# A hybrid decoder layer on one core: experts by four instead of two, half units of w_xo, and four moves in the order of the work

## The chip, the cores and the metric

The kernel is one program on one of the eight cores of a Trainium2 chip, written by hand: each engine (PE, which multiplies matrices; DVE, ACT and POOL, which work on elements; SP, which only issues DMAs here) has its own list of instructions, and they wait for each other by semaphores. The metric is the device time of one execution in microseconds (us), lower is better.

## The reference

One layer of a decoder over 256 tokens of width 1024, everything in fp32, then a last RMS norm:

```python
u = rms_norm(x);  proj = u @ w_in        # 8936 columns: z, xBC, dt, q, k, v, indexer, two gates
y_ssm = ssm_branch(...) @ w_ssm_out      # conv, chunked scan of 32 heads, gated norm with silu(z)
y_att = dsa_branch(...) @ w_att_out      # top 64 keys per query, 16 heads, one k/v head
x = x + (sigmoid(g_ssm) * y_ssm + sigmoid(g_att) * y_att) @ w_mix_out
x = x + cross_attention(rms_norm(x), rms_norm(mem), w_xq, w_xkv, w_xo)    # 4 heads, 256 memory rows
# experts: top 1 of 4 groups, top 2 of its 8 experts, for each token; 32 experts of 1024 x 512
for e in range(32):
    hid = silu(t @ w_e_gate[e]) * (t @ w_e_up[e])
    out = out + comb[:, e:e + 1] * (hid @ w_e_down[e])
x = x + out;  return rms_norm(x)
```

The weights of the experts are 32 x 3 x 2 MB, 201 MB of the 278 MB that the kernel reads.

## The kernel before

**Projections.** Each weight matrix outside the experts comes in units of 128 x 2048 fp32 (1 MB). A unit lands in one of 5 slots of `raw_w`, ACT copies it rounded into one of 3 slots of `hi_w` (L657), DVE subtracts and leaves the rest over the raw values in `lo_w` (L1005), and PE makes three products of the parts (`product`, L1577 to L1579). SP issues a unit when PE has left the one five before it; ACT splits when PE has left the one three before it. The list `units` is the order of the loads, the list `steps` the order of the products. A step is either feature-major (`fm_step`: 256 moving columns) or token-major (`tm_steps`: 512 columns, two tiles of tokens, used for mo, vx and xo, each in two column halves c). Steps alternate between PSUM banks 0 and 1 (`bank_no`), so a step waits until its second forerunner has been evacuated.

**The stages, in order:** k and small projections, convolutions and q, z with the attention, g (gates) with the scan of the heads, ao (attention out), so (scan out), kx, mo, vx, qx, the cross attention, xo, the router, the experts, the last norm.

**The gate stage.** In block b of 16, PE makes g_b, then the weighted sums of heads 2b and 2b+1 (L1763, L1764) with the masked decays `mdec`, which POOL multiplies (L631) after ACT's exponentials (L855). DVE adds the skip term (`y_out`), POOL multiplies with silu(z) (`gate_y`), ACT squares (`square_y`) and splits (`gated_hi`), DVE splits (`gated_lo`). PE sums four blocks of squares at a time with four matmuls on 32 columns of its array each (`sum_squares`, L1806). Behind the last block ACT squares and splits 14 and 15 and makes the sigmoid of the gates (L878), for which the first evacuation of ao (`att_gate`, L1273) waits. The normalised memory rows are turned by PE (`transposes_of(memn, i)`, L1591) inside ao, after steps 4 and 6.

**The experts.** `CAP = 64` token slots per expert and pass. A gather (L1990, L1974) multiplies the normalised rows with one-hot columns `S` for four experts at a time (a turn). A pair of experts is one step: gate and up (`first_layer`, L2007) with two matmuls on 64 array columns each, one per expert, beside each other; silu and product on ACT and DVE (L953, L1521); transposes (L2061); down (`second_layer`, L2038); then the result is split and added to the tokens' rows by `scatter` (L2024). If an expert has more than CAP tokens, DVE counts more passes (`passes`, L1488), and then all weights are loaded and used again. A group is half of one matrix for the two experts of a pair: two pieces of 1 MB, 96 groups in all. The ring has 9 slots of two pieces and one that is used once, made of regions that other stages have left. SP issues the first 20 pieces one by one when their regions are free (among them `over_ring`, which waits for the last unit in a slot), and each later one when PE has left the group nine turns before it (`group_used`).

## Time and profile before

| | us |
|---|---|
| median of three runs | 967.01 (966.19 to 968.02) |
| the profiled execution, its time | 967.55 |
| the profiled execution, its span | 965.80 |
| PE busy | 905.9 |
| DVE, ACT, POOL busy | 445.0, 315.7, 139.1 |
| moved by DMA | 277.61 MB |

The span is from the first to the last recorded instruction. Busy times of one engine are shares of that span; engines overlap. PE's busy time counts pipelined matmuls, which overlap each other too. An "idle before" is the time in which an engine had nothing running in front of an instruction, and behind it stands who released it. Where a row of a table of stages gives busy times, they are of PE, PEld (PE's weight loads), DVE, ACT and POOL, in this order; a granted clock of 1.00 is 2.4 GHz.

### The profile page before, as it was taken

What the parts mean: (1) busy time and instruction counts of PE and PEld (TensorE: products, weight loads), DVE (VectorE), ACT (ScalarE), POOL (GpSimd) and SP (SyncE); (2) the same over time, 40 slices, a digit from 0 to 9 for tenths busy, and PEclk for the clock granted to TensorE, in tenths of its full rate; (3) what the DMA queues carried; (4) which work ended last, traced back from release to release, by engine and by line L of the source; (5) the groups of instructions that cost most, each with busy time, mean ns of one, the idle gap of its engine ahead of it and who ended that gap; (6) DMA issues with size and microseconds to landing.
All of it is one profiled execution on the core that took longest, in us unless ns stands there. A gap on an engine that the chain in (4) does not pass through costs nothing.

```text
span 965.8 us, 13766 instructions
## 1 busy us (share of the span) xinstructions
PE 905.9 (94%) x5671; PEld 624.6 (65%) x5671; DVE 445.0 (46%) x801; ACT 315.7 (33%) x515; POOL 139.1 (14%) x131
## 2 busy tenths in 40 slices
PE   5999999998999999999998999999999988998896
PEld 5899998887889999788774433434343433433432
DVE  4899977677977763464453111212121211210212
ACT  5555676667675334454340000000000000000112
POOL 1002369837850000000000000000000000000000
PEclk9999999999999999999999999999999999999999
DMA  8655553344355769656289899999999999999994
GB/s 225 185 178 172 175 160 110 126 132 131 111 162 152 227 207 359 224 190 246 60 329 362 355 422 421 421 421 421 421 420 421 421 422 420 421 421 421 420 421 184
DMA packets 108728, 277.61 MB, mean 287 GB/s; under 512 B 12850, under 2 KB 76514, under 8 KB 84090
## 3 DMA queue, kind: packets, MB, share of 16 engines
q1 hardware_dynamic: 108522, 276.21, 75.7%
q8 instruction: 45, 0.74, 0.3%
q10 hardware_dynamic: 144, 0.52, 0.1%
q14 instruction: 17, 0.14, 0.0%
HBM read 275.54 MB, written 1.05 MB: 286 GB/s over the span
## 4 chain that ended last, share of the span: by engine, by line
PE 62%; DMA 12%; DVE 7%; SPq 7%; ACT 5%; POOL 4%; issue 3%; ACTq 0%; DVEq 0%; POOLq 0%
PE bank L2007 14%; DMA moe<-in_w_e_up_dram 11%; PE bank L1577 9%; PE bank L1579 9%; PE bank L1578 9%; PE bank L2038 8%; SPq L417 7%; DVE lo_w L1005 2%; PE bank L2024 2%; PE bank L1974 2%; ACT hi_w L657 2%; POOL work L631 2%; PE bank L1763 1%; DVE work L1181 1%; PE bank L1882 1%
## 5 line engine op out<-in xcount | busy, mean ns | idle before, releaser
L2007 PE MATMUL bank<-moe,xg 128*64 128x512 f32 x1008 | 224.9, 595 | 15.3 <-DMA moe<-in_w_e_up_dram 9.9
L1005 DVE TENSOR_TENSOR lo_w<-raw_w,hi_w 128x2048 fp32r<-128x2048 f32 (+1 forms) x68 | 156.8, 2311 | 60.6 <-ACT hi_w L657 60.2
L1577 PE MATMUL bank<-u_hi,hi_w 128*128 128x256 f32 x616 | 177.0, 287 | 0.3 <-DVE work L1182 0.3
L1579 PE MATMUL bank<-u_hi,lo_w 128*128 128x256 f32 x616 | 174.0, 283 | 0.0
L2007 PEld LDWEIGHTS bank<-moe,xg 128*64 128x64 f32 x1008 | 73.7, 137 | 149.5 <-issue 148.8
L1578 PE MATMUL bank<-u_lo,hi_w 128*128 128x256 f32 x552 | 156.0, 283 | 0.0
L657 ACT ACTIVATE hi_w<-raw_w 128x2048 fp32r<-128x2048 f32 (+1 forms) x68 | 127.7, 1880 | 32.5 <-PE bank L1579 29.5
L1577 PEld LDWEIGHTS bank<-u_hi,hi_w 128*128 128x128 f32 x616 | 117.8, 191 | 3.8 <-issue 3.4
L2038 PE MATMUL bank<-moe,moe_buf 128*64 128x512 f32 x512 | 114.3, 596 | 5.9 <-DVE xg L1501 4.7
L1579 PEld LDWEIGHTS bank<-u_hi,lo_w 128*128 128x128 f32 x616 | 117.9, 191 | 0.0
L961 ACT ACTIVATE y_pair_hi<-bank 128x512 fp32r<-128x512 f32 x32 | 19.1, 598 | 291.3 <-PE bank L2038 291.3
L1578 PEld LDWEIGHTS bank<-u_lo,hi_w 128*128 128x128 f32 x552 | 105.6, 191 | 0.0
L2038 PEld LDWEIGHTS bank<-moe,moe_buf 128*64 128x64 f32 x512 | 36.2, 137 | 74.5 <-issue 68.6
L1532 DVE TENSOR_TENSOR y_pair_lo<-bank,y_pair_hi 128x512 fp32r<-128x512 f32 x32 | 22.1, 692 | 116.9 <-ACT y_pair_hi L961 116.9
L1521 DVE SCALAR_TENSOR_TENSOR moe_buf<-moe_buf,st,bank 128x512 f32<-128x512 f32 x16 | 12.0, 747 | 110.6 <-PE bank L2007 103.5
L1509 DVE CAST ST<-bank 128x256 fp32r<-128x256 f32 x16 | 6.8, 425 | 104.2 <-PE bank L2016 104.2
L953 ACT ACTIVATE moe_buf<-bank 128x512 f32<-128x512 f32 x16 | 9.6, 597 | 128.2 <-PE bank L2007 128.2
L631 POOL TENSOR_TENSOR work<-work,cbm 128x384 f32<-128x384 f32 x32 | 40.4, 1284 | 12.5 <-ACT work L855 11.7
L1577 PE MATMUL bank<-a_hi,hi_w 128*128 128x256 f32 x128 | 36.7, 287 | 1.1 <-DVE gates L1273 1.1
L1577 PE MATMUL bank<-y_hi,hi_w 128*128 128x256 f32 x128 | 36.3, 284 | 0.0
L1578 PE MATMUL bank<-y_lo,hi_w 128*128 128x256 f32 x128 | 36.2, 283 | 0.0
L1579 PE MATMUL bank<-y_hi,lo_w 128*128 128x256 f32 x128 | 36.2, 283 | 0.0
(326 smaller groups left out, 1401.2 us busy)
## 6 DMA issues: line engine op xcount, KB each, us to landing
moe<-in_w_e_up_dram SPq DMA_DIRECT2D x64, 1024.0 KB, 26.0
moe<-in_w_e_down_dram SPq DMA_DIRECT2D x64, 1024.0 KB, 26.4
moe<-in_w_e_gate_dram SPq DMA_DIRECT2D x62, 1024.0 KB, 26.0
raw_w<-in_w_in_dram SPq DMA_DIRECT2D x34, 1024.0 KB, 5.5
raw_w<-in_w_ssm_out_dram SPq DMA_DIRECT2D x8, 1024.0 KB, 5.5
raw_w<-in_w_xkv_dram SPq DMA_DIRECT2D x8, 1024.0 KB, 6.3
raw_w<-in_w_att_out_dram SPq DMA_DIRECT2D x4, 1024.0 KB, 5.1
raw_w<-in_w_mix_out_dram SPq DMA_DIRECT2D x4, 1024.0 KB, 8.8
```

The lines of the kernel that those rows point to most:

```text
L417: sp.dma_start(moe_slot[s][a][:, :].rearrange("p (t n) -> p t n", t=t // 2), src)\
L631: nc.gpsimd.tensor_tensor(mdec[:, 2 * ((b + 1) % 2) + a, :], seg[:, 2 * (b % 2) + a, :], cbm[:, h // 8, :], ALU.mult).then_inc(m_ready, 1)
L657: nc.scalar.activation(hi_w[:, m % HI_RING, 0:w], raw_w[:, m % RING, 0:w], ACT.Copy)\
L1005: tt(lo_w[:, m % RING, 0:w], raw_w[:, m % RING, 0:w], hi_w[:, m % HI_RING, 0:w].bitcast(F32), ALU.subtract).then_inc(lo_done, 1)
L1532: tt(y_pair_lo[:, c, :], bank[2 + c][:, :], y_pair_hi[:, c, :].bitcast(F32), ALU.subtract).then_inc(m_ylo, 1)
L1577: mm(dst, left[0], right[0], start=first, stop=False)
L1578: mm(dst, left[0], right[1], start=False, stop=False)
L1579: return mm(dst, left[1], right[0], start=False, stop=last)
L1974: last = mm(bank[b0 + q % 2][:, 256 * (k % 2):256 * (k % 2) + 256], part[:, i, k, :], S[:, i, :, :], start=(i == 0 and part is xn_hi), sto ...
L2007: last = mm(ps[64 * a:64 * a + 64, :], xg[:, k, P * o + CAP * a:P * o + CAP * a + CAP], w[:, k % (KT // 2), :], start=(k == 0), stop=(k == ...
L2024: last = mm(acc_bank[i][c][:, :], ST[o][:, i, :], y[:, c, :], start=False, stop=False, skip_group_check=True)
L2038: last = mm(bank[2 + c][64 * a:64 * a + 64, :], hT[:, k, CAP * a:CAP * a + CAP], w[:, k % 2, 512 * c:512 * c + 512], start=(k == 0), stop= ...
```

## The change

- `CAP` is 32; four experts (a quad) are one step, each on 32 columns of PE's array; a turn is eight experts. A group is half a matrix for four experts, four pieces of 1 MB; there are 48. The ring counts single pieces: 18 slots and two used once, over the same regions.
- w_xo comes in eight half units (256 rows, 512 columns, 512 KB) that share two slots of `raw_w` and two of `hi_w`. The other three slots and one go to expert pieces before the second four half units are issued.
- The weighted sums of block b follow g_(b+1); `y_out`, `gate_y`, `square_y`, `gated_hi`, `gated_lo` and `sum_squares` each come a block later.
- The sigmoid of the attention's gates comes ahead of the last three squares. The sums of squares' end, the memory rows' norm and their transposes come later in ao and behind so0.
- The column halves c=1 of mo, vx and xo go to banks 4 and 5.

The diff, cut:

```diff
-CAP = 64
-PAIRS = EXPERTS // 2
+CAP = 32
+FOUR = P // CAP
+QUADS = EXPERTS // FOUR
+TURN = 2 * FOUR
...
 RING = 5
 HI_RING = 3
 N_PRM = 14
...
         conv_no = {s: n for n, s in enumerate(convolved)}
-        bank_no = [(n - CONV_0) % 4 if CONV_0 <= n < STEP["z0"] else n % 2 for n in range(len(steps))]
+        bank_no = [(n - CONV_0) % 4 if CONV_0 <= n < STEP["z0"] else 4 + n % 2 if s[:3] in ("mo1", "vx1", "xo1") else n % 2
...
                     LAST_STEP[f"{kind}{j}"] = f"{kind}{2 * j + 1}"
+        XO = len(units)
+        for c in range(2):
+            for q in range(4):
+                src = w_xo[0, 256 * q:256 * q + 256, 512 * c:512 * c + 512].rearrange("(t p) n -> p t n", p=P)
+                units.append((f"xo{c}{q}", src, 2))
...
+        def slots_of(n):
+
+            if n < XO:
+                return n % RING, n % HI_RING, 0
+            m = n - XO
+            return (XO + m // 2 % 2) % RING, (XO + m // 2 % 2) % HI_RING, UNIT // 2 * (m % 2)
+
...
+        def before_of(n, ring):
+
+            if n < XO:
+                return n - ring
+            return n - 4 if n >= XO + 4 else XO - ring + (n - XO) // 2
...
+            c, q = divmod(n - XO, 4)
+            if n < XO:
+                eng.wait_ge(proj_ready, STEP[LAST_STEP[units[n][0]]] + 1)
+            elif q < 3:
+                eng.wait_ge(xo_used, 3 * c + q + 1)
+            else:
+                eng.wait_ge(proj_ready, STEP[f"xo{c}1"] + 1)
+
+        OVER_RAW = ((12,), (13,), (10,), (11,), (14,))
+        OVER_HI = ((15,), (6,), (7,))
+        OVER_QX = (19,)
 
         block = ctx.enter_context(nc.Block())
...
+            def over_raw(slot):
+
+                wait_used(sp, max(n for n in range(len(units)) if slots_of(n)[0] == slot))
+                first_load(*OVER_RAW[slot])
+
+            def over_hi(slot):
+
+                wait_used(sp, max(n for n in range(len(units)) if slots_of(n)[1] == slot))
+                first_load(*OVER_HI[slot])
+
             for n, (name, src, k) in enumerate(units):
+                if n == XO + 4:
+                    for slot in range(XO + 2, XO + RING):
+                        over_raw(slot % RING)
+                    over_hi((XO + 2) % HI_RING)
+                    sp.wait_ge(xs_ready, NT * X_HEADS)
+                    first_load(*OVER_QX)
...
-            over_ring(5, 1, raw_slot=3)
-            sp.wait_ge(xs_ready, NT * X_HEADS)
-            first_load(9, 1)
-            over_ring(7, 0, raw_slot=4)
-            over_ring(6, 0, raw_slot=0)
-            over_ring(3, 1, hi_slot=2)
-            over_ring(6, 1, raw_slot=1)
-            over_ring(7, 1, hi_slot=0)
-            over_ring(3, 0, hi_slot=1)
-            over_ring(5, 0, raw_slot=2)
-            first_load(8, 0)
-            first_load(8, 1)
...
+            for k in range(2):
+                over_raw((XO + k) % RING)
+                over_hi((XO + k) % HI_RING)
+            first_load(16)
+            first_load(17)
...
-                turn = turn_of(g) - MOE_RING
-                sp.wait_ge(group_used, turn + 1 if turn < TENTH else turn + 2)
-                for a in range(2):
-                    load_part(turn_of(g) % MOE_RING, a, 2 * (g // 6) + a, *load_of(g // 6, g % 6))
+            first_load(18)
+            for p in range(MOE_RING + len(ONCE), FOUR * MOE_GROUPS):
+                before = turn_of(p) - MOE_RING
+                before = before if before < ONCE[0] else before + len(ONCE)
+                sp.wait_ge(group_used, before // FOUR + 1)
+                first_load(p)
...
-                    gate_y(b - 1)
-            gate_y(SSM_HEADS // 2 - 1)
+                if b >= 2:
+                    gate_y(b - 2)
+            for b in range(SSM_HEADS // 2 - 2, SSM_HEADS // 2):
+                gate_y(b)
 
...
-                square_y(b - 2)
                 if b >= 3:
-                    gated_hi(b - 3)
+                    square_y(b - 3)
+                if b >= 4:
+                    gated_hi(b - 4)
             split_hi_through(UN["ao0"] + 2)
+            wait_evac(act, "g15")
+            nc.scalar.activation(gates[:, 8:16, :], gates[:, 8:16, :], ACT.Sigmoid).then_inc(gsig, 1)
+            square_y(13)
+            gated_hi(12)
             square_y(14)
             gated_hi(13)
             square_y(15)
-            wait_evac(act, "g15")
-            nc.scalar.activation(gates[:, 8:16, :], gates[:, 8:16, :], ACT.Sigmoid).then_inc(gsig, 1)
             gated_hi(14)
...
+            transposed_hi(u_hi, tiles=(0,))
...
+                if b == 1:
+                    transposed_hi(u_hi, tiles=(1,))
...
-                if b >= 1:
-                    y_out(b - 1)
+                if b >= 2:
+                    y_out(b - 2)
                 if b % 2 == 0:
                     split_lo_through(UN[f"g{b // 2}"] + 2)
-                if b >= 4:
-                    gated_lo(b - 4)
+                if b >= 5:
+                    gated_lo(b - 5)
+            y_out(14)
+            split_lo_through(UN["ao0"] + 2)
             y_out(15)
-            split_lo_through(UN["ao0"] + 2)
-            for b in range(12, 16):
+            for b in range(11, 16):
...
                 att_gate(b)
-                if b == 1:
+                if b == 3:
 
                     dve.wait_ge(ssq_mm, 4)
                     nc.vector.tensor_copy(rs_bc, bank[2][:, 0:SEQ]).then_inc(ssq_rows, 1)
-                if b == 2:
+                if b == 4:
+                    norm_rows(1, memx, memn)
+                if b == 5:
                     dve.wait_ge(ssq_mm, 5)
                     link(ts_(rs_bc, bank[2][:, SEQ:2 * SEQ], 1.0 / (32 * D_INNER), EPS, ALU.mult, ALU.add))
                     nc.vector.reciprocal(rs_bc, rs_bc).then_inc(gn_ms, 1)
-                if b == 3:
-                    norm_rows(1, memx, memn)
-                if b == 5:
-                    columns_of(0, g_mem, u_hi, m_lo)
-                if b == 7:
-                    columns_of(1, g_mem, u_hi, m_lo)
+            columns_of(0, g_mem, u_hi, m_lo)
...
+                if b == 0:
+                    columns_of(1, g_mem, u_hi, m_lo)
...
-            split_lo_through(UN["vx10"])
+            split_lo_through(UN["vx11"])
...
+            def state_sums(b):
+
+                pe.wait_ge(m_ready, 2 * b + 2)
+                if b >= 2:
+                    pe.wait_ge(y_used, b - 1)
+                else:
+                    pe.wait_ge(pv_lo, 7 + b)
+                for a in range(2):
+                    h = 2 * b + a
+                    last = weighted_sum(bank[6 + b % 2][64 * a:64 * a + 64, :], xdt[:, 0, HEAD * h:HEAD * h + HEAD],
+                                        xdt[:, 1, HEAD * h:HEAD * h + HEAD], mdec[:, 2 * ((b + 1) % 2) + a, :])
+                last.then_inc(y_ready, 1)
...
-                                        xdt[:, 1, HEAD * h:HEAD * h + HEAD], mdec[:, 2 * ((b + 1) % 2) + a, :])
-                last.then_inc(y_ready, 1)
-                if b in (6, 10, 14):
-                    sum_squares((b - 6) // 4)
-
+                    state_sums(b - 1)
+                if b in (7, 11, 15):
+                    sum_squares((b - 7) // 4)
+            state_sums(15)
 
             for b in range(8):
                 if b % 2 == 0:
                     w = use_unit(f"ao{b // 2}")
                 fm_step(f"ao{b}", w, P * (b % 2), a_parts)
-                if b == 1:
+                if b == 3:
                     sum_squares(3)
...
+                if b == 5:
                     pe.wait_ge(ssq_rows, 1)
                     mm(bank[2][:, SEQ:2 * SEQ], ones[:, :], rs_bc, start=True, stop=True).then_inc(ssq_mm, 1)
-                if b == 4:
+                if b == 7:
                     pe.wait_ge(gn_ms, 1)
                     transposes_of(memn, 0)
-                if b == 6:
-                    transposes_of(memn, 1)
 
...
                 w = use_unit(f"so{b}")
                 fm_step(f"so{b}", w, 0, y_parts, 16)
+                if b == 0:
+                    transposes_of(memn, 1)
 
             pe.wait_ge(tr_evac, 8)
...
 
-            for c in range(2):
-                tm_steps("mo", c, a_parts, mix_lo, (4, 8))
+            tm_steps("mo", 0, a_parts, mix_lo, (4, 8))
+            pe.wait_ge(seg_ready, 32)
...
+            def cross_output(c):
+
+                for q in range(4):
+                    w = use_unit(f"xo{c}{q}")
+                    pe.wait_ge(xo_lo, 2 + q // 2 * 2)
+                    if c == 1 and q == 2:
+                        for i in range(NT):
+                            rows_turned(0, i)
+                    for i in range(NT):
+                        if q == 0:
+                            bank_of(f"xo{c}{i}")
+                        for k in range(2):
+                            last = product(bank[bank_no[STEP[f"xo{c}{i}"]]][:, :],
+                                           [x[:, 2 * q + k, P * i:P * i + P] for x in a_parts],
+                                           [x[:, k, :] for x in w], q == 0 and k == 0, q == 3 and k == 1)
+                        if q == 3:
+                            last.then_inc(proj_ready, 1)
+                    if q < 3:
+                        last.then_inc(xo_used, 1)
+
...
+                    places = [where(off + h, a) for a in range(FOUR)]
+                    for s, landed_at in places:
+                        pe.wait_ge(moe_landed[s], landed_at)
                     for k in range(KT // 2 * h, KT // 2 * h + KT // 2):
                         if rows_at is not None and k in rows_at:
                             pe.wait_ge(m_xg, rows_at[k])
-                        for a in range(2):
-                            w = moe_slot[s][a][:, :].rearrange("p (t n) -> p t n", t=KT // 2)
-                            last = mm(ps[64 * a:64 * a + 64, :], xg[:, k, P * o + CAP * a:P * o + CAP * a + CAP],
-                                      w[:, k % (KT // 2), :], start=(k == 0), stop=(k == KT - 1))
+                        for a in range(FOUR):
+                            w = moe_piece[places[a][0]].rearrange("p (t n) -> p t n", t=KT // 2)
+                            last = mm(ps[CAP * a:CAP * a + CAP, :], xg[:, k, P * o + CAP * a:P * o + CAP * a + CAP],
```

## Rows read from the trace of the kernel before

**Rows 1.** The page's slices, 24.1 us each: what the DMAs moved.
```profile
GB/s 225 185 178 172 175 160 110 126 132 131 111 162 152 227 207 359 224 190 246 60 329 362 355 422 421 421 421 421 421 420 421 421 422 420 421 421 421 420 421 184
```

**Rows 2.** Stages: from:to, length, busy (count) per engine, granted clock, DMA share, GB/s.
```profile
463.50:495.90 32.40, 30.99 (x146) 25.46 (x145) 14.47 (x26) 10.57 (x18) 0.00 (x0) 1.00 0.41 144
495.90:511.70 15.80, 15.21 (x92) 11.26 (x90) 11.97 (x35) 8.02 (x10) 0.00 (x0) 0.89 1.01 417
511.70:545.00 33.30, 30.92 (x149) 12.04 (x150) 7.74 (x32) 2.39 (x4) 0.00 (x0) 1.00 0.85 332
545.00:951.00 406.00, 383.09 (x1872) 166.03 (x1870) 74.70 (x143) 27.86 (x45) 0.00 (x0) 1.00 1.01 420
```

**Rows 3.** SP in order of time: start, length, DMAs issued.
```profile
515.34 4.24 SPq L417 DMA_DIRECT2D moe<-in_w_e_down_dram  x4
...
523.07 11.98 SPq L417 DMA_DIRECT2D moe<-in_w_e_gate_dram  x4
```

**Rows 4.** The chain that ended last: start, length, what.
```profile
915.71 27.06 DMA moe<-in_w_e_up_dram
...
952.80 3.67 PE bank L2038 x16
```

**Rows 5.** Line 417, which issues the expert pieces: time to landing.
```profile
DMA to landing us min/median/max: 5.0/26.1/29.6
```

**Rows 6.** PE in order of time, four places.
```profile
241.34 0.64 PE L1806 MATMUL bank<-work,ones 128*32 128x256 f32 x8
...
506.01 1.10 PE L1949 MATMUL bank<-xres,ident 128*128 128x512 f32 x2
...
511.65 7.09 PE L2007 MATMUL bank<-moe,xg 128*64 128x512 f32 x32
...
528.01 0.75 PE L2061 MATMUL bank<-ident,moe_buf 128*128 128x128 f32 x4 [1.55 <-DVE moe_buf L1521]
```

**Rows 7.** PE in order of time, after the 14th pair.
```profile
899.56 0.39 PE L1974 MATMUL bank<-S,xn_hi 128*128 128x256 f32 x1 [2.71 <-DVE S L1407]
...
903.66 0.28 PE L1974 MATMUL bank<-S,xn_lo 128*128 128x256 f32 x1
```

**Rows 8.** Table of stages as in rows 2, four more stretches.
```profile
213.00:281.00 68.00, 63.97 (x539) 55.45 (x535) 57.05 (x120) 47.07 (x85) 55.86 (x45) 1.00 0.34 109
300.00:350.00 50.00, 50.00 (x419) 49.94 (x418) 36.33 (x47) 19.38 (x18) 0.00 (x0) 1.00 0.64 190
475.00:485.00 10.00, 10.00 (x46) 8.28 (x45) 3.94 (x3) 3.50 (x5) 0.00 (x0) 1.00 0.39 125
900.00:905.00 5.00, 5.00 (x31) 4.93 (x29) 2.08 (x3) 0.00 (x0) 0.00 (x0) 0.66 1.01 421
```

**Rows 9.** What PE waited for: total us, times, longest us.
```profile
PE bank L1763 <- POOL work L631: 3.8, 5, 1.5
...
PE bank L1577 <- DVE xres L1314: 2.5, 3, 0.8
...
PE bank L1591 <- issue: 1.5, 1, 1.5
...
PE bank L1577 <- DVE lo_w L1005: 0.5, 1, 0.5
```

**Rows 10.** ACT and PE between g15 and ao2, in order of time.
```profile
283.68 1.28 ACT L878 ACT_TABLE_LOAD   x1
...
284.97 1.92 ACT L878 ACTIVATE gates<-gates 128x2048 f32<-128x2048 f32 x1
...
288.68 0.36 PE L1577 MATMUL bank<-a_hi,hi_w 128*128 128x256 f32 x1 [1.11 <-DVE gates L1273]
```

**Rows 11.** Issues by line: size, us to landing.
```profile
xdt<-in_mem_dram SPq DMA_DIRECT2D x2, 512.0 KB, 4.2
```

**Rows 12.** Groups, xo stage: busy us, mean ns of one, idle before.
```profile
L1005 DVE TENSOR_TENSOR lo_w<-raw_w,hi_w 128x2048 fp32r<-128x2048 f32 x2 | 4.6, 2292 | 3.7 <-ACT hi_w L657 3.7
...
L657 ACT ACTIVATE hi_w<-raw_w 128x2048 fp32r<-128x2048 f32 x2 | 3.8, 1905 | 0.0
```

More of the change, by code:

```diff
@@ L391, in hybrid_block, with landed_sem @@
         FIRST_STEP.update({f"so{j}": f"so{j}" for j in range(8)})
-        FIRST_STEP.update({f"{k}{j}{h}": f"{k}{j}{h}" for k in ("vx", "mo", "xo") for j in range(2) for h in range(2)})
+        FIRST_STEP.update({f"{k}{j}{h}": f"{k}{j}{h}" for k in ("vx", "mo") for j in range(2) for h in range(2)})
+        def landed_sem(n):
+            return landed[n % RING] if n < XO else xo_landed[(n - XO) % 4]
         def landed_value(n):
+            if n >= XO:
+                return 16 * ((n - XO) // 4 + 1)
             return 16 * (n // RING + 1) + (16 * (len(PIECES[n % RING]) - 1) if n % RING < len(PIECES) else 0)
@@ L652, in split_hi_through, with transposed_hi @@
                     m = split[0]
-                    act.wait_ge(landed[m % RING], landed_value(m))
+                    act.wait_ge(landed_sem(m), landed_value(m))
                     if m >= HI_RING:
-                        wait_used(act, m - HI_RING)
-                    w = unit_len(m)
-                    nc.scalar.activation(hi_w[:, m % HI_RING, 0:w], raw_w[:, m % RING, 0:w], ACT.Copy)\
-                        .then_inc(hi_done, 1)
+                        wait_used(act, before_of(m, HI_RING))
+                    nc.scalar.activation(hi_at(m), raw_at(raw_w, m), ACT.Copy).then_inc(hi_done, 1)
                     split[0] += 1
             group = [0]
-            def transposed_hi(dst, between=None):
-                for i in range(NT):
+            def transposed_hi(dst, between=None, tiles=range(NT)):
+                for i in tiles:
                     for q in range(2):
@@ L1622, in tm_steps @@
                         pe.wait_ge(sem, halves[half])
-                    if half == 1 and between is not None:
-                        between()
                     for i in range(NT):
```

251 lines of the change are left out of this document (124 added, 127 removed).

## The prediction

> **What bounds the kernel now.** I read the busy slices of the page first, then the table of stages, then what PE waited for, then the two ends of the expert stage in order of time. The slices show the DMA rate: uneven between 60 and 359 GB/s in the first 21, and 420 to 422 from the 24th to the 39th [rows 1]. So there are two programs in one. Until about 511.7 us PE is the bound: it is busy nearly all the time and the DMA share is low, except in the last 16 us before the experts, where the ring of expert weights is filled at 417 GB/s. From 545 to 951 us the DMA engines are full (share 1.01, 420 GB/s) [rows 2], whatever PE does. A piece of expert weights is 1.0486 MB, so at 420.5 GB/s one lands every 2.494 us; there are 32 x 3 x 2 = 192 of them, before and after.
>
> That gives the end as a sum of three terms. T0 is when PE begins the first expert (511.65 [rows 6]). The ring holds 20 pieces, all issued by then; the other 172 can only start when PE gives a slot back, first at 515.34 [rows 3]. The last piece: the chain shows the third half-group from the end landing at 915.71 + 27.06 = 942.77, four pieces later is 952.8, and PE starts its last half-group at 952.80 [rows 4]. From there to the end of the span are 13.0 us.
> From 515.34 to 952.8 are 437.5 us for 172 x 2.494 = 428.9 us of transfer. The rest is 8.5 us: 2.5 us are the latency of one piece (its shortest landing is 5.0 us [rows 5], less 2.5 of transfer), and about 6.1 us are DMA engines idle for want of a free slot. The stage 511.7 to 545 shows it: 332 instead of 420 GB/s for 33.3 us is 7.0 us short, some of it before 515.34 [rows 2]. PE is the cause: two half-groups of two experts take 7.09 us (x32), then it waits 1.55 us for the product, and SP sits until 535 over four pieces [rows 3, 6].
>
> **The change part by part.**
> *Experts by four.* The number of matmuls stays, but each drives 32 columns of the array, not 64, and four can run beside each other. What the rows say on that: alone, an fp32 matmul over the whole array and 512 moving columns is two instructions in 1.10 us, some 0.9 without the drain; of those on 64 columns, 16 (x32) take 7.09, 0.443 each. So two do run beside each other, a pair in 0.886. Four 32-column ones already exist: the squares' sums at 241.34, four matmuls of 256 moving columns in 0.64 us with the drain [rows 6]. One after another they would take 4 x 0.44 = 1.8 us. So four run together, and I take 4 x 0.886 = 3.55 us for a half-group of four experts, the time that two experts had. The other end is two by two, 7.1 us.
> The Trainium skill's page TensorE: Matmul & The Clock Gate (part 3, measured speedup) has three column tiles at 2.38 times one, not 3; by that ratio a half-group would be 4.5 us and the result some 2 us later. The row of the four sums is the better witness here.
> In the steady part this buys nothing: PE needs for four experts 4 x 3.55 + 7.1 for the layers, some 5 for slots, transposes and scatters, and a gather of 3.9 every second time, about 28 us in 59.8 of DMA. Where PE was nearly as slow as the DMA, it now has half its time over. At the start it buys the idle time: at T0 + 3.7 as before, but then four slots (10 us of transfer) come free for every 3.6 us of PE. SP never starves again: ring 18, four pieces landed and in work, 14 outstanding, minus 1.5 landed before the next four are issued. **-6.1 us**, bounds -6.1 and 0.
> *The tail.* PE will now wait some 6 us before each half-group (10 us of DMA, 3.6 of work). After 2.71 us of idle time at 899.56 the granted clock was 0.66 over the next 5 us [rows 8], and the gather's matmuls took about 0.4 instead of 0.28 until about 903.5 [rows 7]: about 4 us at the 1.2 GHz level. While DMA is the bound that is free: even a whole half-group at half rate is 7.1 us, under 10. But the last one is behind the last piece: 4 us at half rate do 2 us of work, the rest 1.6: 5.6 instead of 3.6, **+2.0 us**; bounds 0 and +5.5 (all of it and the scatters at half rate).
> That an idle PE falls to the lower clock is also what the Trainium skill says (TensorE: Matmul & The Clock Gate, part 1, HAM oscillation); by that rule this change, which makes PE idle by design, pays at the end, and the row agrees.
> *Weighted sums a block later.* PE waited 3.8 us for POOL's product in the gate stage [rows 9]. POOL is busy 55.9 of 68 us there [rows 8], so it is no bound, only late by a part of a step; one more fm step (24 matmuls at 50/419 us, 2.9 us [rows 8]) in front covers the longest wait (1.5). Left open by it is the end of the stage: the last sums stand bare behind g15, y_out(15) stands behind a split of w_att_out, and the chain ACT split 1.9, table load 1.3, sigmoid 1.9, the squares and copies of 13 to 15 (seven at about 0.45), DVE's last lows and att_gate(0), 0.9, is 9.0 us [rows 10, 12]; PE's work between g15 and ao2 is 7.3 (sums 0.9 and 0.6, two steps of 2.9), so the wait of 1.1 becomes about 1.7, though the sigmoid now comes first: DVE waits for the last lows all the same. Of 3.8 + 1.1 + the short 0.4 I keep 0.7 in the blocks and 1.7 here: **-2.9 us**, bounds 0 and -5.3.
> *Memory rows turned later.* The 1.5 us before L1591 [rows 9] was the chain square root, scaling, transposes; it now has two to three more ao steps. **-1.5 us**, bounds 0 and -1.5. The second half behind so0 lies in 5.8 us steps and delays nothing.
> *Second halves in banks 4 and 5.* Three waits of 0.8 us for a residual addition (the rows' 2.5 [rows 9]) go, in mo, vx and xo; the new wait for seg_ready is long past. With the split of vx11 ahead of the columns the 0.5 us for lo_w goes too. **-3.0 us**, bounds 0 and -3.0.
> *Half units of w_xo.* Eight loads of 512 KB in place of four of 1024; c=1 reuses the slots of c=0, so each is issued when PE has left its forerunner. PE spends 12 x 10/46 = 2.6 us on a half unit [rows 8], so a load has three of them, 7.8 us. It needs a landing (512 KB of mem: 4.2 us [rows 11]), ACT's copy (half of 1.9) and DVE's subtraction (half of 2.3) [rows 12]: 6.3, slack 1.5. ACT and DVE sit on the half units with the norm's squares and the residual additions queued behind them; for xo12 the additions then come at the moment PE wants them for the transposes. I take **0**, bounds 0 and +4 (1 us for each of four). What it buys is five expert pieces issued before the second half rather than after; the ring was full at T0 anyway, so this only protects the smaller T0.
> *Router and tables.* Later passes have seven entries, not three, and the slot weights four copies: about 1.5 us more on DVE, which had 3 us to spare before the first slots are turned. Nothing.
>
> Sum: -2.9 - 1.5 - 3.0 = -7.4 on T0, -6.1 behind it, +2.0 at the end: -11.5. The profiled execution took 967.55 us (span 965.80), the median of the three runs is 967.01; so 967.55 - 11.5 = 956.05, less 0.54: **955.5 us**.
>
> **Rivals.** (1) *PE's gains before T0 are given back*: POOL and DVE at 82 and 84% of the gate stage become the pace, or the w_xo half units come late. For it: DVE's busy time there is 57.1 of 68 [rows 8]. Then -7.4 becomes -1 to -3: 960 to 962. (2) *The lower clock holds through the end*: +5.5 instead of +2.0, 959. Against it: the row recovers in about 4 us of work. (3) *Four tiles run two by two*: half-groups take 7.1 us, the 6.1 us stay lost and the last half-group costs 3.6 more, so 967.0 - 7.4 + 3.6 + 3 for the later first release: about 966, no change. Against it: the 0.64 us. (4) *A second pass, the slower side*: a pass now serves 32 tokens of an expert, not 64, and one expert with 33 makes every weight come again: 192 x 2.494 = 479 us, so 1434 us. It decides at one token: routing the reference's own inputs (its default draw) gives 512 places over 32 experts, 16 on average, and the busiest has exactly 32; another draw has 33. The nearest token outside that expert is 0.09 away in a logit whose spread is 7, far over what split fp32 loses, so I hold it unlikely, but nothing else here costs so much. (5) *More than forecast*: no clock loss, and all waits gone, 951 to 953.
>
> **How the numbers follow.** Forecast, from 952 to 959: 0.70. Rival 1: 0.12, rival 2: 0.06, rival 3: 0.03, rival 4: 0.03, rival 5: 0.06. The range that leaves out under 2 in 10 is 951.5 to 961. A measurement here tells 0.2% (1.9 us): faster 0.95 (all but rivals 3 and 4 and a rest), the same 0.02, slower 0.03.
>
> **What would show it.** Right: the gate stage without POOL in PE's waits; banks 4 and 5 without residual waits; T0 near 504; full DMA rate from about T0 + 6; half-groups of x32 in 3.6 to 5.6 us with waits of 4 to 6 us for DMA ahead of them; a granted clock well under 1.00 among the experts; 192 expert loads. Wrong: 7 us for x32 at full clock; waits for lo_w in the xo stage; 384 loads.

## The result, and the profile after

The changed kernel takes **962.07 us** (median of 6 runs, 961.76 to 963.32), beside 967.25 for the kernel before on the same chip (966.19 to 969.27): ratio 0.995, 95% interval 0.994 to 0.9961. The forecast was 955.5, with a range of 951.5 to 961.0. So it is faster, as forecast, but by 5.2 us where 11.5 were worked out, and the time lies outside the range. The profiled execution has a span of 959.9 us at a mean granted clock of 0.905.

The page's slices, of 24.0 us each, answer to [rows 1]; above the DMA rate stands the TensorE clock in tenths:
```profile
PEclk9999999999999999999999888776887777887787
...
GB/s 222 190 176 176 162 155 125 132 132 133 132 173 180 175 243 358 206 166 295 101 296 309 421 422 421 422 421 421 421 421 421 421 422 421 421 421 422 420 421 169
```
The full DMA rate now begins a slice earlier, with the 23rd, and from slice 23 on the clock is no longer at its upper level. The table of stages of the kernel after (columns as in [rows 2]) and what PE waited for:
```profile
511.70:545.00 33.30, 23.43 (x210) 7.77 (x202) 6.31 (x33) 1.79 (x3) 0.00 (x0) 0.96 0.95 389
...
650.00:900.00 250.00, 155.99 (x945) 54.01 (x941) 23.52 (x50) 9.31 (x15) 0.00 (x0) 0.79 1.01 421
```
```profile
PE bank L2094 <- DMA moe<-in_w_e_up_dram: 60.3, 14, 6.4
PE bank L2094 <- DMA moe<-in_w_e_gate_dram: 54.5, 13, 6.3
PE bank L2126 <- DMA moe<-in_w_e_down_dram: 44.0, 12, 6.3
...
PE bank L1652 <- DVE work L1100: 4.4, 1, 4.4
...
PE bank L1959 <- DVE work L1427: 3.4, 3, 1.4
```
PE waits 159 us for expert pieces, where it was idle for only 23 of 406 us [rows 2]; that was meant. The fourth row shown was not: 4.4 us in one wait, on work that DVE does ahead of the transposes of xn1. POOL, at the head of [rows 9], is gone from the list.

PE and the queue in order of time (start, length, what; in brackets the idle time before it and what ended it), at the places that answer to [rows 3, 4, 6]:
```profile
412.81 1.94 PE L1652 MATMUL bank<-ident,ysT 128*128 128x128 f32 x8 [4.36 <-DVE work L1100]
...
493.82 0.66 PE L1993 MATMUL bank<-ident,xres 128*128 128x128 f32 x4 [0.96 <-DVE xres L1372]
...
508.88 4.06 PE L2094 MATMUL bank<-moe,xg 128*32 128x512 f32 x34
...
516.60 7.07 PE L2094 MATMUL bank<-moe,xg 128*32 128x512 f32 x64
```
```profile
493.30 21.73 SPq L467 DMA_DIRECT2D moe<-in_w_e_down_dram  x7
```
```profile
918.36 27.18 DMA moe<-in_w_e_down_dram
945.67 4.97 PE bank L2126 x32
```
The experts begin at 508.88, 2.8 us earlier, where 7.4 were forecast. Two half-groups of four experts (x64) take 7.07 us, as long as two half-groups of two experts took [rows 6]: four column tiles do run beside each other. The last half-group takes 4.97 us, mostly at the lower clock.

The table shows all kernels of this study, in us, with the span cut at four marks; each row is one profiled execution. The first mark, PE's first product on the low part of the memory rows (the stage of keys for the cross attention), falls between 350.8 and 352.2 in the kernels with the changed gate stage, which is the spread of one execution against another.

| kernel | mark to last transposes of xres | to T0 | to last half-group | tail |
|---|---|---|---|---|
| before (mark 356.31) | 140.3 | 15.0 | 441.2 | 13.0 |
| after (351.81) | 142.0 | 15.1 | 436.8 | 14.3 |
| vx10_split (352.00) | 138.8 | 15.0 | 436.9 | 14.3 |
| vx11_between (350.92) | 136.9 | 14.6 | 436.7 | 14.7 |
| vx11_between_mean (350.75) | 136.3 | 15.0 | 437.1 | 15.7 |
| all_four (351.72) | 136.3 | 16.6 | 437.1 | 13.0 |
| all_four_again (350.88) | 136.2 | 14.6 | 437.3 | 13.0 |
| sums_same_block (355.81) | 142.2 | 15.1 | 436.5 | 14.5 |
| experts_by_two (350.90) | 143.5 | 16.7 | 440.4 | 13.0 |
| warm_tail (351.97) | 142.2 | 15.1 | 436.7 | 13.0 |
| vx11_wait_filled (351.71) | 140.7 | 16.6 | 436.7 | 14.3 |
| before_vx11_split (355.80) | 143.6 | 16.7 | 441.4 | 13.0 |
| second_halves_parity (350.96) | 145.7 | 16.7 | 437.1 | 14.7 |
| ring_filled_late (352.18) | 136.9 | 16.6 | 436.9 | 14.6 |

After against before: the first mark is 4.5 us earlier, the next stretch 1.7 longer, the router (to T0) the same, the ring (from T0 to the last half-group) 4.35 shorter, the tail 1.3 longer: -5.8, the difference of the spans.

### The profile page after: what moved, and what is told of

The parts are those of the page before. It is cut to its first block, busy times and chain, and to the rows that moved or that the text cites. A ratio compares the mean times of both kernels' runs of the same rounds, so it can differ in the third digit from the quotient of the medians.

```text
span 959.9 us, 13117 instructions
## 1 busy us (share of the span) xinstructions
PE 762.4 (79%) x5399; PEld 542.5 (57%) x5399; DVE 407.4 (42%) x753; ACT 302.8 (32%) x495; POOL 140.7 (15%) x131
## 4 chain that ended last, share of the span: by engine, by line
PE 43%; DMA 36%; DVE 7%; ACT 5%; SPq 4%; issue 3%; POOL 2%; ACTq 0%; DVEq 0%
DMA moe<-in_w_e_down_dram 14%; DMA moe<-in_w_e_gate_dram 13%; PE bank L1638 10%; PE bank L1640 9%; PE bank L1639 9%; DMA moe<-in_w_e_up_dram 8%; PE bank L2094 5%; SPq L467 4%; ACT hi_w L713 3%; DVE lo_w L1064 2%; PE bank L2126 2%; PE bank L1822 1%; PE bank L1948 1%; PE bank L1725 1%; POOL qiT L624 1%
## 5 line engine op out<-in xcount | busy, mean ns | idle before, releaser
L2094 PE MATMUL bank<-moe,xg 128*32 128x512 f32 x1008 | 166.4, 814 | 114.8 <-DMA moe<-in_w_e_up_dram 60.3
L2094 PEld LDWEIGHTS bank<-moe,xg 128*32 128x32 f32 x1008 | 44.3, 143 | 228.2 <-issue 227.7
L2126 PE MATMUL bank<-moe,moe_buf 128*32 128x512 f32 x512 | 73.2, 725 | 46.4 <-DMA moe<-in_w_e_down_dram 44.0
L1021 ACT ACTIVATE y_pair_hi<-bank 128x512 fp32r<-128x512 f32 x16 | 9.6, 597 | 278.8 <-PE bank L2126 278.8
L2126 PEld LDWEIGHTS bank<-moe,moe_buf 128*32 128x32 f32 x512 | 20.7, 130 | 94.3 <-issue 92.3
L1582 DVE SCALAR_TENSOR_TENSOR moe_buf<-moe_buf,st,bank 128x512 f32<-128x512 f32 x8 | 6.0, 748 | 135.6 <-PE bank L2094 128.8
L1593 DVE TENSOR_TENSOR y_pair_lo<-bank,y_pair_hi 128x512 fp32r<-128x512 f32 x16 | 11.1, 692 | 118.9 <-ACT y_pair_hi L1021 118.9
L1569 DVE CAST ST<-bank 128x256 fp32r<-128x256 f32 x8 | 3.4, 425 | 128.4 <-PE bank L2104 128.4
L1013 ACT ACTIVATE moe_buf<-bank 128x512 f32<-128x512 f32 x8 | 4.8, 597 | 152.0 <-PE bank L2094 152.0
L687 POOL TENSOR_TENSOR work<-work,cbm 128x384 f32<-128x384 f32 x32 | 37.8, 1204 | 13.0 <-ACT work L910 12.3
```

Of the source, the lines that this page charges most:

```text
L687: nc.gpsimd.tensor_tensor(mdec[:, 2 * ((b + 1) % 2) + a, :], seg[:, 2 * (b % 2) + a, :], cbm[:, h // 8, :], ALU.mult).then_inc(m_ready, 1)
L1021: nc.scalar.activation(y_pair_hi[:, c, :], bank[2 + c][:, :], ACT.Copy).then_inc(m_yhi, 1)
L1593: tt(y_pair_lo[:, c, :], bank[2 + c][:, :], y_pair_hi[:, c, :].bitcast(F32), ALU.subtract).then_inc(m_ylo, 1)
L2094: last = mm(ps[CAP * a:CAP * a + CAP, :], xg[:, k, P * o + CAP * a:P * o + CAP * a + CAP], w[:, k % (KT // 2), :], start=(k == 0), stop=(k ...
L2126: last = mm(bank[2 + c][CAP * a:CAP * a + CAP, :], hT[:, k, CAP * a:CAP * a + CAP], w[:, k % 2, 512 * c:512 * c + 512], start=(k == 0), st ...
```

## The experiments

**Where T0's gain went: DVE's order at vx11.** ACT and DVE of the kernel after, in order of time, ahead of the 4.36 us:
```profile
407.83 1.90 ACT L713 ACTIVATE hi_w<-raw_w 128x2048 fp32r<-128x2048 f32 x1
```
```profile
407.48 0.76 DVE L1393 TENSOR_SCALAR ysT<-xres,st 128x1024 f32<-128x1024 f32 x1 [0.27 <-ACT st L763]
409.77 2.29 DVE L1064 TENSOR_TENSOR lo_w<-raw_w,hi_w 128x2048 fp32r<-128x2048 f32 x1 [1.53 <-ACT hi_w L713]
411.98 1.28 DVE L1100 TENSOR_TENSOR work<-bank,prm 128x512 f32<-128x512 f32 x2
```
DVE stands in order: vx11's split waits for ACT's copy, and the columns, whose first multiplications free the banks that PE wants, wait behind the split. The experiment undoes that one line:
```diff
-            split_lo_through(UN["vx11"])
+            split_lo_through(UN["vx10"])
             columns_of(0, g_x, a_hi, a_lo, NT)
```


> The changed kernel with one line of it undone: ahead of the columns of xn1, DVE splits the units up to vx10 again, not up to vx11. Theory (the gain before T0 was lost in DVE's queue): vx11's split waits there for ACT's hi copy and stands ahead of the four columns, so that PE waited 4.36 us (at 412.81) for the transposes of xn1. Undone, that wait falls to about 0.5, 0.5 us for lo_w come back behind it, T0 moves from 508.9 to about 505, and since the DMA engines stand idle from about 507 to 513.7 in the changed kernel the 4 us pass to the end one to one: 958 us, against 962.1. Rival (the loss before T0 is in the half units of w_xo or elsewhere): the wait only moves, T0 stays within 1 us of 508.9 and the time at 961 to 962. Second rival (the ring cannot use an earlier T0): T0 goes to 505 and the end stays at 962.

Measured: 959.04 us (957.64 to 959.94), ratio to before 0.9927 (0.9914 to 0.9941), T0 at 505.83, last landing with it (436.9 behind it). PE of this kernel:
```profile
409.17 1.22 PE L1652 MATMUL bank<-ident,ysT 128*128 128x128 f32 x8 [0.53 <-DVE work L1100]
...
417.50 0.50 PE L1638 MATMUL bank<-hi_w,u_hi 128*128 128x512 f32 x1 [1.63 <-DVE lo_w L1064]
```
The theory holds, both rivals fall: 3.05 us of T0 went into this line, and they pass to the end. But 1.63 us for lo_w come back, not 0.5: with bank waits gone PE is earlier, and vx11's split, now last, is late by more.

> The kernel before with only this line of the change: DVE splits the units up to vx11, not vx10, ahead of the columns of xn1. Theory: the four columns stand behind a split that waits for ACT's hi copy; PE's wait ahead of the transposes of xn1 grows from 0.43 us to about 4.4, 0.5 us for lo_w go, T0 moves from 511.65 to about 515, and the time from 967.2 to 970.5 or 971. Rival (in the kernel before, ACT's copy is earlier against DVE, and the line costs only where the second halves have banks of their own): under 1 us, 967 to 968.

The line alone in the kernel before (the opposite edit there): 969.51 us (968.9 to 972.16), ratio 1.0037 (1.0023 to 1.0051), and 143.6 us from the mark to the transposes against 140.3. So it costs 3.2 us there too, a wait of 3.11 and slower work behind it. The rival falls; T0 (516.02) is 1.0 us later than expected: the router took 1.6 us more (below), and this execution was 0.5 us ahead at the first mark.

The split can stand between, in columns_of behind the first tile's multiplications by the gain:
```diff
-            split_lo_through(UN["vx11"])
-            columns_of(0, g_x, a_hi, a_lo, NT)
+            split_lo_through(UN["vx10"])
+            columns_of(0, g_x, a_hi, a_lo, NT, between=UN["vx11"])
...
+                        if ii == i and q == 1 and between is not None:
+                            split_lo_through(between)
```


> The changed kernel, and DVE's split of vx11 neither ahead of the columns of xn1 (as in the changed kernel) nor behind them (as with the line undone), but between them: after the first tile's two multiplications by the gain, where DVE waited 1.35 us for ACT's a_hi in the run with the line undone (409.6 to 410.97), and where ACT's hi copy of vx11 is just done (409.9). Theory (with banks of their own the second halves wait for nothing but lo_w, and DVE's order is all that is left): neither the 4.36 us of the changed kernel nor the 1.63 us for lo_w of the undone line; the wait ahead of xn1's second transposes stays 0.5; T0 near 504.2 against 505.8 with the line undone, time 957.4. Rival (DVE has no room: a_lo or the splits of qx0 come late instead): a wait of 1 to 2 us moves to qx0 near 421 and the time stays at 959.

Measured: **956.04 us** (955.66 to 959.01), ratio 0.9894 (0.9877 to 0.991). DVE:
```profile
407.26 1.28 DVE L1100 TENSOR_TENSOR work<-bank,prm 128x512 f32<-128x512 f32 x2
408.88 2.29 DVE L1064 TENSOR_TENSOR lo_w<-raw_w,hi_w 128x2048 fp32r<-128x2048 f32 x1 [0.34 <-ACT hi_w L713]
411.08 0.69 DVE L1088 TENSOR_TENSOR a_lo<-work,a_hi 128x512 fp32r<-128x512 f32 x1
```
Neither the 4.36 nor the 1.63 us are left, and no wait comes at qx0. From the mark to the transposes it is 136.9 us against 142.0: **the place of one DVE instruction was worth 5.1 us.** Other profiles repeat both: 136.9 in ring_filled_late, 142.2 in sums_same_block and warm_tail. (T0, 502.47, is 1.7 earlier than expected: 1.1 of it because this execution was ahead from the first mark on, 0.4 in the router.)

**The wait costs more than itself.** In every kernel with the 4.36 us the granted clock falls behind it. Stages of the kernel after, then of the one with the line undone:
```profile
412.00:416.00 4.00, 3.19 (x12) 2.93 (x13) 3.69 (x7) 1.86 (x3) 0.00 (x0) 0.57 0.19 63
```
```profile
412.00:416.00 4.00, 3.87 (x18) 2.86 (x16) 3.79 (x6) 2.75 (x3) 0.00 (x0) 1.00 0.24 81
```
To tell the wait from the small transposes behind it, PE gets something to do in it:
```diff
-            transposes(xn1)
+            transposes_of(xn1, 0)
+            for _ in range(4):
+                mm(bank[6][:, :], ones[:, :], xres[:, 0, 0:512], start=True, stop=True, skip_group_check=True)
+            transposes_of(xn1, 1)
```


> The changed kernel, and PE runs four fp32 matmuls (ones on 512 columns of xres into bank 6, which nobody reads) between the transposes of xn1's two tiles, in the 4.36 us in which it waits for DVE. Nothing else is changed: DVE's order and the wait's end stay. Theory (the wait costs more than itself: in every kernel that has it the granted clock is 0.5 to 0.76 in the 2 to 5 us behind it, and the eight transposes take 1.94 us, not 1.22, while with the line undone the clock stays at 1.00): the transposes take 1.22 us, the clock stays at 1.00, and T0 comes some 1.1 us earlier than 508.9: 961. Rival (the low clock there comes from the transposes' own small matmuls): the same 1.94 us and T0 unchanged, 962.

```profile
408.19 3.60 PE L1931 MATMUL bank<-xres,ones 128*128 128x512 f32 x8
412.71 1.22 PE L1652 MATMUL bank<-ident,ysT 128*128 128x128 f32 x8 [0.92 <-DVE work L1100]
```
The transposes take 1.22 us and the clock stays at 1.00; from the mark to the last transposes it is 140.7 against 142.0. So the idle time, not the small matmuls, lowers the clock, and that costs 1.3 us here. The time, 962.83 us (959.47 to 963.68), ratio 0.995, does not show it, so it rests on the traces: in the profiled execution T0 is 509.03, because its router took 1.6 us more.

**Experts by four.**
```diff
-CAP = 32
+CAP = 64
```


> The changed kernel with CAP = 64: two experts on two times 64 columns again, sixteen pairs, all else of the change kept. Theory (the trace of the changed kernel gives experts by four 4.35 us less between T0 and the last landing, and 1.2 us more behind it): T0 stays at 508.9 within 0.5 us, a half-group of two experts is 7.1 us per x32 at full clock, the granted clock among the experts is back near 1.00, idle time of the ring returns, and the end comes 3 us later: 965.2 us. Rival (experts by four bring nothing net; all of the gain is T0's): 962. Second rival (they bring my forecast 6.1 - 2.0 = 4.1 us or more): 966.2 or above.

Measured: 964.32 us (962.18 to 966.11), ratio 0.9975 (0.9965 to 0.9984). From T0 to the last half-group it is 440.4 us, not 436.8, and the tail 13.0, not 14.3: experts by four are worth 3.6 - 1.3 = 2.3 us, and the ratios, 0.9975 and 0.995, differ by 2.4. The mean granted clock is back at 0.987. The theory's size was 3.1 us; T0 was not 508.9 but 511.02: 1.45 us more behind the vx wait and 1.6 more in the router, both at the lower clock, less 0.9 at the first mark. Both rivals fall.

> The changed kernel, and in the last four experts alone PE runs six matmuls on ones and hT into bank 5, which nobody reads, between the second last half-group and the last one, where it waits some 6 us for the last pieces. Theory (the tail is longer because an idle PE is granted the 1.2 GHz level): the last half-group (x32 at 945.67) takes about 3.6 us, not 4.97, and the time falls by 1.3 us to 960.8. Rival (the 4.97 us are not the clock's, but four tiles one beside another at the end): it stays at 4.9 and the time at 962; second rival (the dummies are still running when the last pieces land): as much as 1 us later than 962.

The edit of warm_tail, in the second layer of the last four experts:
```diff
+                    if h == 0 and keep_busy:
+                        for _ in range(6):
+                            mm(bank[5][:, :], ones[:, :], hT[:, :, :], start=True, stop=True, skip_group_check=True)
```
```profile
939.60 5.42 PE L2134 MATMUL bank<-moe_buf,ones 128*128 128x512 f32 x12
945.90 3.64 PE L2126 MATMUL bank<-moe,moe_buf 128*32 128x512 f32 x32 [0.88 <-DMA moe<-in_w_e_down_dram]
```
3.64 us, not 4.97, and a tail of 13.0, as before the change: the longer tail is the clock's and nothing else's. 960.67 us (960.28 to 962.92), ratio 0.9948; beside 0.995 for the kernel after the time alone would not have shown it.

**Weighted sums.** The gate stage in the old order, in the kernel after (PE's part stands here; POOL's gate_y, ACT's squares and high parts, DVE's y_out and low parts move forward by one block likewise, the sigmoid stays first):
```diff
-                else:
-                    state_sums(b - 1)
-                if b in (7, 11, 15):
-                    sum_squares((b - 7) // 4)
-            state_sums(15)
+                state_sums(b)
+                if b in (6, 10, 14):
+                    sum_squares((b - 6) // 4)
```


> The changed kernel with the gate stage in the order of the kernel before: PE's weighted sums of block b in block b, and POOL's products, y_out, squares, gated hi and lo one block earlier; the sigmoid stands after both squares' halves as changed. Theory (the forecast's 2.9 us were right, the trace of the changed kernel has ao start 4.1 us earlier and so start 5.4 earlier than before, of which 1.5 is the memory rows'): PE waits for POOL's product come back in groups of 0.5 to 1.5 us, 3.8 in sum, the 1.5 us at ao2 go partly, and T0 moves from 508.9 to about 511.8: 964.5 to 965. Rival (the sums a block later bring nothing: the end of the stage pays them back): within 1 us of 962.

Measured: 966.34 us (965.39 to 970.61), ratio 1.0001 (0.999 to 1.0012); by the ratios, all that the whole change gains is gone: 4.9 us, give or take 1.5. The profiled span is 4.15 us longer than after's. What PE waited for between 205 and 345 us, in it and then in the kernel after:
```profile
PE bank L1817 <- POOL work L687: 3.9, 6, 1.5
PE bank L1633 <- DVE gates L1327: 2.3, 2, 1.7
```
```profile
PE bank L1638 <- DVE gates L1332: 2.2, 2, 1.5
PE bank L1822 <- DVE ysT L1282: 0.3, 1, 0.3
```
The first mark is at 355.81 against 351.81: 4.0 us, where I had 2.9. The 2.2 for the gates are there in both orders, so the sums do not pay for them; I had charged them with 0.6 (1.1 before, 1.7 expected).

**Banks 4 and 5.** On top of the mended order:
```diff
-        bank_no = [(n - CONV_0) % 4 if CONV_0 <= n < STEP["z0"] else 4 + n % 2 if s[:3] in ("mo1", "vx1", "xo1") else n % 2
+        bank_no = [(n - CONV_0) % 4 if CONV_0 <= n < STEP["z0"] else n % 2 if s[:3] in ("mo1", "vx1", "xo1") else n % 2
```


> The kernel with vx11's split between the columns, and the second halves of mo, vx and xo again in banks 0 and 1 (their additional waits stay). Theory (with DVE's order mended the banks are worth what was forecast for them): the waits for a residual addition of 0.8 us come back ahead of mo1 and xo1, and one for ACT's evacuation ahead of vx1; T0 2 to 2.4 us later than 502.5 and 958.3 us. Rival (the additions and the splits of the next unit end together, so that banks alone are worth nothing; as with the line undone, where 1.63 us for lo_w came in place of 0.83 + 0.50): within 0.7 us of 956.

Measured: 966.55 us (964.0 to 967.05), ratio 0.9989 (0.9979 to 0.9999): 9 us more than with the banks (0.9894), and the stretch from the first mark to the last transposes is 8.8 us longer. Theory and rival both miss. PE and then DVE of this kernel:
```profile
400.52 0.50 PE L1640 MATMUL bank<-hi_w,u_hi 128*128 128x512 f32 x1 [0.84 <-DVE xres L1374]
...
480.49 0.77 PE L1640 MATMUL bank<-hi_w,a_hi 128*128 128x512 f32 x1 [3.65 <-DVE xres L1374]
```
```profile
478.51 1.23 DVE L1064 TENSOR_TENSOR lo_w<-raw_w,hi_w 128x1024 fp32r<-128x1024 f32 x1 [1.41 <-ACT hi_w L713]
479.66 1.28 DVE L1374 TENSOR_TENSOR xres<-bank,xres 128x512 f32<-128x512 f32 x2
```
With half units DVE splits through xo12 before it adds the first half's residual, and these splits wait for loads, which wait for PE. With banks shared PE waits 3.65 us for that addition, and the clock is at 0.50 from 480 to 486. With half units and shared banks the stretch is 5.4 us longer than in the kernel before (145.7 against 140.3), with half units and banks of their own 3.4 us shorter. Full units with banks of their own were not run, so the two parts have a price here only as a pair.

**Order in the xo stage.**
```diff
             residual_add("xo", 1, 0)
-            inverse_mean_of_rows(3, 0)
             residual_add("xo", 1, 1)
+            inverse_mean_of_rows(3, 0)
```


> As the run with vx11's split between the columns, and at the end of the xo stage DVE adds both tiles' residuals before it works out tile 0's inverse mean. Theory (the 0.96 us ahead of the last transposes come from three small DVE instructions and their wait for ACT's squares, put between two residual additions that follow each other by 1.36 us now that the last quarter of w_xo holds all the last products): the wait falls to about 0.4, T0 another 0.5 to 0.6 earlier, 956.8. Rival (the sum of squares of tile 0 is on the path to the router's scale): the gain comes back as a wait for DVE in the router, no change.

The wait fell from 0.96 to 0.35, and the mark-to-transposes stretch from 136.9 to 136.3. The time did not show it: 957.17 us (956.58 to 958.29), ratio 0.9902 (0.9887 to 0.9917). In the profiled executions it is not the rival's wait for DVE but the clock that took it: in the router it was low in this one and not in the other, and the last half-group took 6.35 us, not 5.37.

**The early fill of the ring.**
```diff
             for n, (name, src, k) in enumerate(units):
-                if n == XO + 4:
-                    for slot in range(XO + 2, XO + RING):
-                        over_raw(slot % RING)
-                    over_hi((XO + 2) % HI_RING)
-                    sp.wait_ge(xs_ready, NT * X_HEADS)
-                    first_load(*OVER_QX)
...
+            for slot in range(XO + 2, XO + RING):
+                over_raw(slot % RING)
+            over_hi((XO + 2) % HI_RING)
+            sp.wait_ge(xs_ready, NT * X_HEADS)
+            first_load(*OVER_QX)
             for k in range(2):
```


> The kernel with vx11's split between the columns, and SP issues the five pieces of expert weights that the change puts ahead of the second half of w_xo behind it instead (as one would have to with full units). Theory A (the ring's fill is short of its end by about as much as the DMA engines idle before the first release, some 6 us from 502 to 508.5): the fill of 12 pieces ends near 514.4, not 502, the idle time goes, and the last landing comes 12.5 - 6.4 = 6 us later: 962. Theory B (my forecast: the ring is full at T0 anyway, the early issue is worth 0): within 1 us of 956.

Measured: 959.06 us (957.34 to 959.52), ratio 0.9912 (0.9897 to 0.9927); the profile has 436.9 us from T0 to the last half-group, as with the early fill, and T0 at 505.67, of which 1.3 stand at the first mark and 2.0 in the router. Theory A falls as to the ring: the DMA engines are then busy from 480 on, and still 331 GB/s in 510 to 515, but every slot is filled or in flight when the first is given back. In the ring the early issue is worth nothing here, as the forecast had it. The time lies between the two theories, outside both: against vx11_between the ratios say 1.7 us more, give or take 2.2, and behind T0 the two traces are alike (436.9 and 14.6 us against 436.7 and 14.7).

**All together** (split between, additions first, six dummy matmuls ahead of the last half-group).

> As the run before it (split between, additions first), with the six dummy matmuls between the second last half-group and the last. The version that should beat all: T0 about 503.6, the DMA idle before the first release unchanged (its fill ends some 14.5 us after the last xo product, whatever T0), last half-group 3.65 us instead of 4.97: 955.6. Rival (the ring's fill has a fixed end near 507, so that a T0 before 503.5 is worth nothing): 956.5 or more with a last landing that does not follow T0.

> The same kernel as all_four, beside the others on another chip. The low clock in the router lasts 0, 3.4 or 6.8 us in the profiles, and PE reaches T0 14.6, 15.0 or 16.7 us behind the last transposes; by that the time is between 954.3 and 956.7, and the median near 955.5. Rival (the long dip belongs to this kernel): 956.5 again, with the long one in the trace.

Measured: 956.52 us (953.49 to 957.09), ratio 0.9885 (0.9868 to 0.9902), and on another chip **955.71 us** (953.77 to 956.85), ratio 0.9884 (0.9867 to 0.9901): 11.5 us less than the median of before on that chip (967.2), and some 6 less than the change as it was made, by the ratios. The first had the long low clock in the router, the second none (spans 954.7 and 952.0), so it isn't the kernel's. The rival's number for all_four came true, its mechanism not: the last half-group follows T0 by 437.1 us. Against vx11_between alone (956.04) the medians tell no difference, although the tail is 1.7 us shorter in the profiles.

## Why the prediction was wrong

The sum of three terms stands: the difference of the spans is their sum, and the ring's time behind T0 was 436.5 to 437.3 us in all eleven profiles with experts by four, with T0 anywhere from 501.7 to 513.4. Term by term:

- **T0, -7.4 forecast, -2.8 measured. The step that failed is "With the split of vx11 ahead of the columns the 0.5 us for lo_w goes too".** I priced what the edit removes, and did not work out what stands behind the moved instruction on DVE, nor when what it waits for is ready. ACT's copy ends at 409.73, the transposes of the first tile were done at 408.45. With the split between the columns the same change does what the term said: T0 502.5.
- *Second halves in banks 4 and 5, -3.0.* The stretch of mo, vx, qx and xo grew by 1.7 us with the vx11 line. Against before it shrank by 1.5 with the line undone, by 3.4 with the split between the columns, and by 4.0 with the additions first as well. Right in size once the order is, but by a mechanism that I only half saw: with the half units the banks are worth 9 us, not 2.5. I priced the half units at 0 beside banks that I priced by the old waits.
- *Weighted sums, -2.9, and memory rows, -1.5.* Together 4.4 forecast, 4.5 measured at the first mark. Alone 4.0 and 0.5: the wait of 1.5 us for the rows' transposes went, but 0.65 us at so0 and 0.4 more at ao2 (both DVE, with or without the sums) took its place. Their cause I did not try apart. The 0.5 is not clear of the spread: before_vx11_split, with the gate stage of before, has the mark at 355.80, where sums_same_block has 355.81. So the memory rows were worth 0 to 0.5 us, where 1.5 were forecast, and the sums more than the 2.9 forecast for them: luck made the sum of the two come out.
- **The ring, -6.1 forecast, -4.35 measured**, is a term mis-sized: the failed part is "2.5 us are the latency of one piece". From SP's first issue into a freed slot (512.58, T0 + 3.7 as forecast) to PE's last half-group (945.67) are now 433.1 us for 172 pieces of 2.494: 4.1 us are left, with the DMA engines full (419 to 424 GB/s) from 515 to 940. I had taken 2.5 for that remainder, from the shortest landing, and so counted 1.6 us of it as idle time that the change would save; the other 0.1 is a slip of the sum, 8.5 - 2.5 being 6.0. Most of the remainder lies at the start: the first piece lands 5.3 us after its issue, 2.8 more than its transfer, and the third lands 3.5 us behind the second, 1.0 more. Why the third is late was not tried. experts_by_two gives 3.6 us for experts by four alone; the other 0.8 came with the rest of the change, most likely the issue piece by piece, which I did not try by itself.
- **The tail, +2.0 forecast, +1.3 measured** (up to +2.7 in other executions: 6.35 us for the last half-group). Mechanism right, shown by warm_tail.
- The rivals: the first named about the right sum (960 to 962 from T0's gains given back) and the wrong place, POOL, DVE's load or late w_xo; PE waited for none of these. The missing one was a queue, not a load: DVE was 49% busy from 352 to 485 us. One pass of 192 loads, and four tiles at once, as forecast.

So of the 6.6 us between 955.5 and 962.07, 4.6 are T0's and 1.75 the ring's, less 0.7 of the tail. The other 0.9: the profiled execution of after took 961.76 us, 0.3 under its median, that of before was 0.5 above its own, and 0.1 is rounding.

## What to carry to other kernels

Before an instruction is moved forward in an engine's order, read when its operand is ready and what stands behind it: here one split, 2.29 us long, ahead of an operand by 1.5 us, cost 5.1 us. Two edits that touch the same waits (smaller load units, separate banks) have a price as a pair; cost the second in the order that the first makes. Where a kernel is made of a stage bound by compute and one bound by transfer, do not take the remainder beside the transfers from one shortest landing: follow the landings behind the first freed slot. Here 2.5 us were taken and 4.1 were there.

## What the runs showed of the hardware

*Four column tiles of fp32.* Sixteen matmuls on 32 columns with 512 moving columns take 3.54 us (x64 in 7.07), eight on 64 columns the same (x32 in 7.09, experts_by_two and [rows 6]): four tiles do twice as many matmuls, each on half as many columns, in the time of two. Four beside each other take 0.885 us, as long as one fp32 matmul on all 128 columns (four in 3.60 us, vx11_wait_filled); one on 32 columns alone was not run. The Trainium skill (TensorE: Matmul & The Clock Gate, part 3, measured speedup) has 2.38 for three column tiles. No run here has three, so the figure itself is not tested; carried over to four, as in the prediction, it gives 4.5 us for a half-group, the trace has 3.54, and the measurement decides.

*The lower clock follows idle time of PE, and in the router also none.* At the end of the 4.36 us of idle time the granted clock falls to 0.50, the 1.2 GHz level, for 3.4 us; filling the wait takes that away. But in the router it falls although PE has had no idle time for 1.9 to 4.2 us. Two stretches of all_four and of vx11_between, the same code, at the same place:
```profile
492.00:496.00 4.00, 4.00 (x10) 2.45 (x10) 2.43 (x16) 3.79 (x3) 0.00 (x0) 0.50 1.01 424
```
```profile
492.00:496.00 4.00, 3.64 (x15) 1.86 (x15) 3.60 (x19) 3.95 (x5) 0.00 (x0) 1.00 1.01 424
```
In the 14 profiles the clock is at 0.50 there for no time (2), 3.4 (6) or 6.8 us (6), and the way to T0 takes 14.6, 15.0 or 16.6 us, in no fixed relation to the kernel (all_four has 16.6 once and 14.6 once). What starts it was not tried. It falls where PE does 32 matmuls of 36 moving columns: among them in seven profiles, within 0.3 us of the last one's start in five. The 2.0 us between the shortest and the longest way are more than three effects that the traces show (1.3, 0.6 and 1.3 us) and that the medians of four to six runs don't. That it is what hides them is likely but not shown, since one execution of each kernel was profiled.
